# A hybrid decoder trunk: the opening, the S5 set-up and the S5 scan arranged in another way

## What is computed

```python
mod = (silu(c) @ ada_w[i] + ada_b[i])      # 6 parts of 1024: shift, scale, gate for mixer and FFN
hn = rms_norm(h, norm_mix_w[i]) * (1 + sc_m) + sh_m
proj = hn @ w_in                           # q, k, v, z, b/a (8 columns), u
# S5: 32 groups of 16 channels, each with 64 complex states
mag = exp(lr * dt); lb = mag * (cos(li * dt), sin(li * dt))
f = (lb - 1) / lam;  bb = f * b            # complex
x_t = lb * x_{t-1} + bb @ u_t              # complex scan over 512 steps
y = Re(c @ x) + d * u;  y = gelu(y);  y = y * sigmoid(y @ glu_w + glu_b)
# GDN: silu(causal conv of q, k, v), l2 norm, chunked delta rule, head norm, * silu(z)
out = concat(o_gdn, y_s5) @ w_out
```

## Time and profile before

| | us |
|---|---|
| runs | 1557.35, 1566.99, 1559.36 (median 1559.36) |
| the profiled execution | 1569.96, its span 1568.4, mean granted clock 0.909 |
| PE busy | 1415.3 (90%) |
| DVE busy | 771.9 (49%) |
| ACT busy | 503.9 (32%) |
| POOL busy | 215.3 (14%) |

### The profile page before, as it was taken

One profiled execution on the slowest core, in us unless ns is written; L12 is line 12 of the kernel. 1 busy time (PEld: TensorE's weight loads), 2 busy tenths in 40 slices (PEclk: granted clock), 3 DMA queues, 4 the chain that ended last, 5 costly groups with the idle time before them and its releaser, 6 DMA issues.

```text
span 1568.4 us, 17805 instructions
## 1 busy us (share of the span) xinstructions
PE 1415.3 (90%) x6956; PEld 1183.2 (75%) x6956; DVE 771.9 (49%) x762; ACT 503.9 (32%) x569; POOL 215.3 (14%) x256
## 2 busy tenths in 40 slices
PE   2479968968997899999999999999986999999997
PEld 1357857857996688888888878888775888888886
DVE  7792884065564646623366552444446323333243
ACT  3225320044413332212222234566524222222232
POOL 5891991034000000000000000000000000000000
PEclk6577985678999899989999979999997999999999
DMA  9117756310011447623374322211122232342321
GB/s 323 50 47 106 228 169 172 81 54 1 1 55 27 134 142 233 227 77 98 107 232 168 109 81 81 81 55 49 33 81 81 80 107 74 93 128 80 87 84 71
DMA packets 205705, 164.12 MB, mean 105 GB/s; under 512 B 29601, under 2 KB 195714, under 8 KB 203602
## 3 DMA queue, kind: packets, MB, share of 16 engines
q1 hardware_dynamic: 202416, 137.25, 30.7%
q0 software_dynamic: 2720, 25.99, 4.6%
q10 hardware_dynamic: 514, 0.12, 0.1%
HBM read 158.23 MB, written 4.19 MB: 104 GB/s over the span
## 4 chain that ended last, share of the span: by engine, by line
PE 78%; POOL 8%; DVE 6%; issue 4%; ACT 3%; DMA 1%; SPq 0%; DVEq 0%; ACTq 0%; POOLq 0%
PE banks L467 21%; PE banks L468 21%; PE banks L469 21%; PE banks L688 4%; DMA ada_first<-in_ada_w_dram 1%; DVE hn_lo L1547 1%; PE banks L659 1%; PE banks L661 1%; PE banks L922 1%; PE banks L949 1%; POOL scan_a L2107 1%; PE banks L663 1%; PE banks L542 1%; POOL scan_a L2108 1%; POOL scan_a L2102 1%
## 5 line engine op out<-in xcount | busy, mean ns | idle before, releaser
L467 PE MATMUL banks<-hn_hi,whi 128*128 128x512 f32 x992 | 393.0, 396 | 5.0 <-DVE hn_lo L1547 4.9
L468 PE MATMUL banks<-hn_lo,whi 128*128 128x512 f32 x992 | 390.6, 394 | 0.0
L469 PE MATMUL banks<-hn_hi,wlo 128*128 128x512 f32 x992 | 389.9, 393 | 0.0
L1515 DVE TENSOR_TENSOR wlo<-raw,whi 128x2048 fp32r<-128x2048 f32 (+3 forms) x107 | 232.0, 2169 | 145.0 <-ACT whi L1103 83.9
L467 PEld LDWEIGHTS banks<-hn_hi,whi 128*128 128x128 f32 x992 | 189.1, 191 | 48.4 <-issue 9.2
L1109 ACT ACTIVATE whi<-raw 128x2048 fp32r<-128x2048 f32 (+1 forms) x66 | 123.1, 1866 | 316.9 <-PE banks L469 315.8
L469 PEld LDWEIGHTS banks<-hn_hi,wlo 128*128 128x128 f32 x992 | 189.1, 191 | 40.2
L468 PEld LDWEIGHTS banks<-hn_lo,whi 128*128 128x128 f32 x992 | 189.3, 191 | 39.0
L467 PE MATMUL banks<-ff_hi,whi 128*128 128x512 f32 x416 | 163.9, 394 | 0.0
L469 PE MATMUL banks<-ff_hi,wlo 128*128 128x512 f32 x416 | 162.7, 391 | 0.0
L468 PE MATMUL banks<-ff_lo,whi 128*128 128x512 f32 x416 | 162.6, 391 | 0.0
(11 more groups left out here) (409 smaller groups left out, 1923.3 us busy)
## 6 DMA issues: line engine op xcount, KB each, us to landing
raw<-in_ffn_w_in_dram SPq DMA_DIRECT2D x88, 512.0 KB, 4.9
ada_in<-in_ada_w_dram POOLq DMA_DIRECT2D x16, 1536.0 KB, 6.4
ada_in<-in_ada_w_dram SPq DMA_DIRECT2D x32, 512.0 KB, 4.1
raw<-in_ffn_w_out_dram SPq DMA_DIRECT2D x32, 384.0 KB, 3.9
raw<-in_sb_w_in_dram SPq DMA_DIRECT2D x24, 512.0 KB, 4.4
raw<-in_hy_w_in_dram SPq DMA_DIRECT2D x20, 512.0 KB, 5.9
raw<-in_ffn_w_out_dram SPq DMA_DIRECT2D x32, 320.0 KB, 3.6
ada_first<-in_ada_w_dram SPq DMA_DIRECT2D x4, 2048.0 KB, 18.6
```

What stands on the lines that cost most here:

```text
L467: pe.matmul(o, lh, rh, start=first, stop=False)
L468: pe.matmul(o, lh, rl, start=False, stop=False)
L469: return pe.matmul(o, ll, rh, start=False, stop=last)
L1515: TTO(wlo[s][:, 0:width], raw[s][:, 0:width], whi[s][:, 0:width].bitcast(F32), SUB)\
```

## The change

1. `lam_raw` (16x128: lam_re, lam_im, dt) is turned by PE at once; DVE does everything on 128x16: 37 small instructions where there were 36 on 16x128, and after the sines another 29 (`lb`, `f`, powers), writing `pw_re`, `pw_im`, `f_co` itself. POOL's 29 instructions, PE's 18 turns and ACT's `powers` are gone. `sq` of x comes after this in DVE's list, and ACT's sines come ahead of its copies of x.
2. `c_raw` is loaded from ACT's queue; PE turns it after x's tile 3, ACT copies it after its tile 3 (`c_parts`). POOL then builds v in 12 instructions of half the size, waits for all of `hn`, zeroes `m_in`.
3. `ada_first` gets four tiles' room for all, 8 DMAs of 1 MB without a wait.
4. DVE makes `bb` right after the squares; after the norm come `w_rows(0, 0)`, `lo(2)`, `w_rows(0, 1)`, `lo(3)`, and `w_rows(1, ...)` between the conv blocks of q.
5. PE: u blocks 0 and 1 together, tile by tile of `hn` (`as_tiles_come`); b/a; u blocks 2, 3; then q's four blocks; then the taps, the gate sums, the 32 turns, p (three banks in turn instead of two); then k's and v's blocks.
6. The scan: each state is turned by a table (`turn_cos`, `turn_sin`, 128x1024 each) so that the recurrence is real; DVE does it in 12 instructions of 128x1024 and 32 `tensor_tensor_scan` of 128x64, in eleven pieces between the conv blocks of k and v. POOL's scan (120 instructions) goes; POOL makes the tables instead.
7. The tables and `scan_a`, `scan_b` lie over `ada0_in`. So SP waits for `scan_done` before tile 16 now, loads tiles 16 to 39, then `u_again`, `y_dram`, `y_s5`, then tiles 40 to 47, then slots 10, 11. DVE takes tiles 16 to 31 after the last conv block.
8. PE: `mod_parts(2)` between the third and fourth group of y, `mod_parts(4)` after both z slots.

```diff
@@ sync
-            for g in range(4):
-                if g == 3:
-                    sp.wait_ge(ada_used, 4)
-                rows = ada_w[0].rearrange("(p t) n -> p t n", t=8)[:, 4 * (g % 2):4 * (g % 2) + 4, :]
...
+            for g in range(8):
...
+            for n in range(4, 6):
+                load_slot(n, n % 2, cols(w, 256 * (n - 2))(n % 2))
             sp.wait_ge(u_out, 64)
-            sp.wait_ge(w_done, 8)
+            sp.wait_ge(v_done, 1)
...
-            for part in range(4, 6):
+            sp.wait_ge(scan_done, 1)
+            for part in range(2, 5):
                 for t in range(8):
                     ada0_tile(part, t)
-            sp.wait_ge(scan_done, 1)
...
+            for t in range(8):
+                ada0_tile(5, t)
             for s in range(2):
                 load_slot(10 + s, s, cols(s5_glu_w[0], 256 * s, k=4)(s))
@@ tensor
+            as_tiles_come(0, B_U, 0, (0, 1), lambda w_: w_[:, :].rearrange("p (k two m) -> p k two m", k=KT, two=2))
...
+            four_blocks(2, B_QKV, hn_hi, hn_lo)
             pe.wait_ge(bb_done, 1)
             pe.wait_ge(v_done, 1)
             for q in range(8):
-                b = 4 + q % 2
+                b = 4 + q % 3
...
-            with pe.Fori(0, 3) as i:
+            with pe.Fori(1, 3) as i:
                 four_blocks(2 + 2 * i, B_QKV + 4 * i, hn_hi, hn_lo)
-            mod_parts(2, ada0_acc, (24, 32))
...
             for q in range(4):
+                if q == 3:
+                    mod_parts(2, ada0_acc, (24, 32))
+                    pe.wait_ge(mod_done, 2)
...
+            z_blocks(0)
+            z_blocks(1)
+            pe.wait_ge(y_done, 4)
+            mod_parts(4, ada0_acc, (40, 48))
@@ scalar
+            act.preload_act_table(ACT.Silu)
+            qkv(0)
+            act.wait_ge(g_abs, 1)
+            step(act.activation(g_t[0][:, :, :], g_t[0][:, :, :], ACT.Exp, scale=-1.0))
+            act.activation(g_t[0][:, :, :], g_t[0][:, :, :], ACT.Ln, bias=ONE_C).then_inc(g_ln, 1)
+            act.activation(beta[:, :, :], ba[:, :, 0:NH], ACT.Sigmoid).then_inc(beta_done, 1)
+            act.wait_ge(m_zero, 1)
+            for q in range(8):
+                act.wait_ge(k_sum, q + 1)
...
@@ vector
+            for src, by, dst, n in ((1, 1, 2, 1), (1, 2, 3, 2), (1, 4, 5, 4)):
...
+            def states_turned(at_):
+                c_, s_ = turn_cos[:, :, :], turn_sin[:, :, :]
+                re, im, a, b = s_re[:, :, :], s_im[:, :, :], scan_a[:, :, :], scan_b[:, :, :]
+                def scans(dst, src, lo_):
+                    for i in range(lo_, lo_ + 8):
+                        last = dve.tensor_tensor_scan(dst[:, i, :], decay[:, i:i + 1].to_broadcast([P, NC]),
+                                                      src[:, i, :], 0.0, MUL, ADD)
+                    step(last)
+                if at_ == 0:
+                    dve.wait_ge(p_done, 4)
+                    dve.wait_ge(turn_done, 1)
+                    step(TTO(a, re, c_, MUL))
...
+                elif at_ == 10:
+                    TTO(re, b, a, SUB).then_inc(scan_done, 1)
...
+            for i in range(1, 3):
                 for r in range(4):
+                    if i == 1 and r == 0:
+                        states_turned(0)
+                    conv_block(i, r)
+                    for at_ in ((1, 2), (3,), (4, 5), (6,), (7,), (8,), (9, 10), ())[4 * i + r - 4]:
+                        states_turned(at_)
+            for part in range(2, 4):
+                for t in range(8):
+                    ada0_tile(part, t)
@@ gpsimd
+            for half in range(2):
+                ii = slice(8 * half, 8 * half + 8)
...
+            pool.wait_ge(hn_done, 8)
             pool.wait_ge(v_done, 1)
             pool.memset(m_in[:, :, :], 0.0).then_inc(m_zero, 1)
...
+            n = 1
+            while n < NC:
+                shape = [P, PAIRS, n]
...
+                step(tt(w_, s0, s_, MUL))
+                step(tt(c1, c0, c_, MUL))
+                step(tt(c1, c1, w_, SUB))
+                step(tt(w_, c0, s_, MUL))
+                step(tt(s1, s0, c_, MUL))
+                last = tt(s1, s1, w_, ADD)
+                n *= 2
+                if n < NC:
+                    step(last)
+                    doubled(turn_n)
+                else:
+                    last.then_inc(turn_done, 1)
```

More of the change, by code:

```diff
@@ L547, in _ @@
             pe.wait_ge(consts, 1)
+            pe.wait_ge(dt_done, 1)
+            for n in range(3):
+                last = pe.transpose(bank[5][:, 16 * n:16 * n + 16], lam_raw[:, n, :], ident[0:16, 0:16])
+            last.then_inc(lam_t, 1)
             pe.wait_ge(x_in, 16 * TT)
@@ L556, in _ @@
                 last.then_inc(x_t, 1)
-            norm(0)
+                if k == 3:
+                    pe.wait_ge(lam_exp, 1)
+                    pe.wait_ge(c_raw_in, 16 * 4)
+                    for part in range(2):
+                        for q in range(4):
+                            last = pe.transpose(bank[4 + part][:, q * P:(q + 1) * P], c_raw[:, part, q, :],
+                                                ident[:, :])
+                    last.then_inc(c_t, 1)
             pe.wait_ge(vec_in, 16 * 8)
@@ L584, in _ @@
             last.then_inc(ba_rows, 1)
-            four_blocks(0, B_U, hn_hi, hn_lo, first=True)
+            slot_ready(1)
+            for j in range(2):
+                gemm(2 + j, 1, j, hn_hi, hn_lo)
             pe.wait_ge(ba_copied, 1)
@@ L1059, in _ @@
             act.wait_ge(lam_in, 48)
-            act.activation(lam[:, 14, 0:2], lam[:, 14, 0:2], ACT.Exp).then_inc(dt_done, 1)
+            act.activation(lam_raw[:, 2, :].rearrange("i (two p) -> i two p", two=2),
+                           lam_raw[:, 3, 0:2].unsqueeze(2).to_broadcast([16, 2, GP]), ACT.Exp).then_inc(dt_done, 1)
+            for part, src in enumerate((s5_c_re, s5_c_im)):
+                rows = src[0].rearrange("(q g) h p -> (g h) q p", q=4)
+                for two in range(2):
+                    act.dma_start(c_raw[:, part, :, 64 * two:64 * two + 64], rows).then_inc(c_raw_in, 16)
             act.dma_start(vec_b[CONV:CONV + 48, :], hy_conv_w[0].rearrange("j (b p) -> (j b) p", p=P))\
@@ L1075, in _, with c_parts @@
             act.activation(c_act[:, :], c_col[:, :], ACT.Silu).then_inc(c_ready, 1)
+            def c_parts():
+                act.wait_ge(c_t, 1)
+                for par in range(2):
+                    rows = slice(64 * par, 64 * par + 64)
+                    for dst, b, scale in ((c_re, 4, 1.0), (nc_re, 4, -1.0), (nc_im, 5, -1.0)):
+                        src = bank[b].rearrange("p (i two h) -> p i two h", two=2, h=GH)[rows, :, par, :]
+                        last = act.activation(dst[rows, :, :], src, ACT.Copy, scale=scale)
+                last.then_inc(c_done, 1)
+            act.wait_ge(lam_exp, 1)
+            act.activation(lam[:, 11, :], lam[:, 8, :], ACT.Sin)
+            act.activation(lam[:, 10, :], lam[:, 7, :], ACT.Sin).then_inc(lam_trig, 1)
             for k in range(KT):
@@ L1619, in _ @@
+            w_rows(0, 0)
+            lo(2, 0)
+            w_rows(0, 1)
+            lo(3, 1)
             dve.wait_ge(ba_sum, 1)
@@ new lines, in conv_block @@
+            def conv_block(i, r):
+                dve.wait_ge(conv_tap, 4 * i + r + 1)
+                for s in range(1, 4):
+                    w_ = CONV + 12 * (3 - s) + 4 * i + r
+                    d_ = conv[:, i, r, s:T]
+                    last = STT(d_, bank[r][:, 0:T - s], vb[:, w_:w_ + 1], d_, MUL, ADD)
+                    if s < 3:
+                        step(last)
+                last.then_inc(block_free, 1)
+                if r == 1:
+                    lo(4 + 2 * i, 0)
+                if r == 3:
+                    lo(5 + 2 * i, 1)
@@ L2001, in _ @@
                         .then_inc(bc_in, 16)
-            for part, src in enumerate((s5_c_re, s5_c_im)):
-                rows = src[0].rearrange("(q g) h p -> (g h) q p", q=4)
-                for two in range(2):
-                    pool.dma_start(c_raw[:, part, :, 64 * two:64 * two + 64], rows).then_inc(bc_in, 16)
             pool.dma_start(w_ba[:, :, :], hy_w_in[0][:, 4 * W:4 * W + 8].rearrange("(k p) n -> p k n", p=P))\
```

488 lines of the change are left out of this document (209 added, 279 removed).

## The result

The changed kernel takes 1581.65 us (median of three runs, 1578.72 to 1584.71) against 1559.36: 1.2% slower, ratio 1.0122 [1.0082, 1.0162]. Forecast were 1567 and a range up to 1582, so the time lies 0.35 us inside the range's upper end, and on the slower side of the 1% bound, to which I had given 0.20. The profiled execution is the one of 1584.71, its span 1583.1.

A forecast was written before the change was run, and what follows sets the result against it. Only the part before the first GDN product can change, where PE waited 21.2 us for POOL's scan. `scan_done` 220.2 + tail 114 = 334 against 326.4, +7.8 us; on the median 1559.36 that gives 1567, range 1542 to 1582.

The forecast's parts named there:

- 1% bound: Whole kernel: slower by over 1%, above 1575 us, was given a chance of 0.20.
- S: The time of `scan_done`, forecast at 220.2 us; the steps behind it are counted from there.
- ACT's `c_parts` lets POOL begin at 29.7: Opening: ACT's copies of c_raw are done so that POOL starts the v build at 29.7 us.
- to 23.2: Opening: DVE's 37 and 29 small steps, 9.3 + 6.4 us from 7.5 on, end at 23.2.
- The port: Opening: POOL's v build and DVE's two-input instructions take turns on the SBUF port, from 29.7 to 64.8 us.
- the rival of a less strict one: Opening: DVE slips in two instructions per POOL instruction, norm up to 15 us sooner, time 1552; chance 0.12.
- p to scan_done: DVE's scan, conv blocks, `lo` and a wait for k: 49.1 us instead of 89.8, `scan_done` at 220.2.
- From the gate step to p: Taps, gate sums, turns and p on PE at the low clock, from 142.8 to `p_done` at 171.1 us.
- The tail: From `scan_done` to the GDN sums: tiles at 2.8 us and the y path on SP's list, 114 us, +28.7.
- The rival "the tiles hide": Behind `scan_done`: a tile takes 1.9 us, the 24 tiles save 22 us, time 1545; chance 0.13.
- The first rival (tables late): POOL's scan tables ready only at 197 us, DVE waits, `scan_done` 21.5 us later, time 1588; chance 0.15.
- a dear scan (+12): DVE's 32 scan instructions, 6.7 us with bounds 4 to 19; the dear case sets the range's high side.

The follow-up runs named there:

- Run 1: The changed kernel with the four c_raw loads moved from ScalarE's queue back to GpSimd's; 1574.74 us, ratio 1.0081 to the kernel before.
- run 3: The changed kernel with GpSimd's v build waiting until the norm is done; 1570.28 us, ratio 1.0039 to the kernel before.
- run 6: The changed kernel with a third buffer for the condition's tiles; 1574.01 us, ratio 1.0057 to the kernel before.
- runs 5 and 12: 5: the changed kernel with all scan steps at once, 1586.1 us. 12: run 11 with two z blocks in front of y, 1532.63 us.
- run 8: The changed kernel itself, measured again as the base; 1582.45 us, ratio 1.0125 to the kernel before.
- run 11: The changed kernel with c_raw on GpSimd's queue, v build behind the norm, third tile buffer, y path behind all tiles; 1539.31 us.

## Why the prediction came out as it did

Step by step, forecast against the profile after:

| step | forecast | measured |
|---|---|---|
| VectorE's powers end | 23.2 | 32.4 |
| v build | 29.7 to 64.8 | 38.6 to 73.2 |
| norm end | 93.5 | 101.3 |
| last u block | 111.3 | 120.7 |
| first `m_in` copy after the gate step | 142.8 | 152.0 |
| `p_done` | 171.1 | 177.8 |
| tables ready | 157 | 157.8 |
| `scan_done` | 220.2 | 226.0 |
| tile 31, 40 used | S + 46, + 87 | S + 45, + 87.5 |
| first sum of squares | S + 114 = 334 | S + 115.9 = 342.0 |

- **The step that failed** is "ACT's `c_parts` lets POOL begin at 29.7", and ahead of it the 66 steps "to 23.2": I let the powers run through without pricing ScalarE's queue, on which the sines stand behind the four c_raw loads. The change moves these DMAs, and I counted them as nothing. Run 1 shows the term: 8 to 9 us, and with it put in, the forecast for the first sum is 342 to 343, against 342.0.
- **The port** was right, and the rival of a less strict one wrong: a tile of 1.28 takes 3.3 beside GpSimd, and the v build took 34.6 us (35.1 forecast). The Trainium skill says in "GPSIMD Engine Reference", in the table at its head, that the SBUF interfaces are shared and contended for where VectorE has two SBUF inputs; run 3 agrees, 3.26 against 1.28 us, and the addition of the squares 2.7 against 0.68. What I did not ask is who needs v: nobody before the taps at 150. The 24 us at the norm, of which 17 are left at `scan_done`, were to be had by one wait, and theory A of run 3 still had the opening set by the powers and the loads.
- **p to scan_done** was 48.3 us against 49.1; the scans 6.3 us against 6.7, the products 1.23 each. From the gate step to p the forecast was 2.5 too long, since the clock was back at 1.00 from 170 us on, where I had taken the low one for all turns. The tables were ready as forecast partly by luck: GpSimd began them 4 us late (101.4 against 97) and took 56.4 us instead of 60.
- **The tail** was right in size and in cause: SyncE's list, tiles at 2.64 to 2.8 us, u_again and y in the middle. The rival "the tiles hide" failed. Its 1.9 us a tile exists, but it takes a third buffer (run 6). The first rival (tables late) didn't occur here; in run 3 it is just reached. Two small sums of the prediction are off, 29.5 less five times 0.6 is 26.5 and not 26.7, and 111.3 + 21.9 is 133.2 and not 133.6; nothing hangs on them.
- **Beyond the profile** there are 22.3 us between the medians where the profiled executions are 14.7 apart. The profiled execution of before was 10.6 above its median, and I took that excess for something the change does not touch. That was an assumption: behind the first sum this profile is as long as all others (1242.0), so the excess may as well lie in front of it, in the stretch that changes. The other executions of before were not profiled and their spread is wide (1553.6 to 1572.0 over the later runs), so the cause of this half of my miss, 7.5 of 14.7 us, stays open.
- **The range** held, and by luck. Its upper end stood on a dear scan (+12), and the scan was slightly cheaper than forecast. What brought the time up there were ScalarE's queue and the 7.5 us between profiles and medians, and neither was among its terms.

In parts: p comes 26.4 us later than before (177.8 against 151.4), from there to `scan_done` 41.5 are won (48.3 against 89.8), and the tail costs 30.6 more (115.9 against 85.3). So the change loses because its gain of 15 us at `scan_done` (23 in run 1, without the queue's term) is smaller than the 31 us of tiles and transfers that it sends behind `scan_done`. With c_raw's queue, the place of the v build, a third buffer and the order behind `scan_done` changed, a kernel with this scan is 2% faster than the one before; how much of that the kernel before would gain from the same edits was not tried.

Not tried either: the mod sum at another place between the y groups, and a y that keeps the full clock beyond its first 5 us (runs 5 and 12).

## What to carry to other kernels

A DMA issue is an instruction of the engine that issues it: price it at the time for which it holds that engine, which here rose from 0.4 to 8.1 us once other loads were ahead of it in the same queue, and look at what stands behind it. Where two engines share a port, ask who needs the slower one's result and start it after the other one's chain, not as early as its inputs allow. And when work is pulled forward in a list with fixed posts (a sum between two groups, transfers between two parts), find the next post first; until it is moved, speed in front of it is worth nothing.

## What was not expected of the hardware

- Two DMAs of 512 packets of 256 bytes each (128 KB) held ScalarE's queue for 8.69 us, and a following one of 24 KB held it for 4.57. The price is not one per load: the first three of the four c_raw loads took 0.40 to 0.54 us, the fourth alone 8.13 (view of the tile `c_raw`, min/median/max ns below). All DMAs together moved some 400 GB/s up to 13 us and 206 to 278 from there to 21. ScalarE's queue carried 2112 more packets than before, 2048 of them c_raw's (behind the tile's row: queue and kind, packets, MB, share; before, then after):

```profile
L1064 ACTq DMA_DIRECT2D c_raw<-in_s_c_im_dram x2: 532/4332/8131, 7.9 to 8.5; - x2
```
```profile
q10 hardware_dynamic: 514, 0.12, 0.1%
```
```profile
q10 hardware_dynamic: 2626, 0.64, 0.2%
```
  From GpSimd's queue the same four took 0.77 to 0.80 us each (run 1). Full DMA engines alone don't make it dear: in run 1 ScalarE's eight small loads took 0.26 to 0.58 us each, between 6.8 and 10 us, while 412 GB/s were moved. Small packets are not needed for it: SyncE's two loads of 512 KB issued at 5.2 us took 7.75 us, and two of the same kind at 104.7 us 0.92. What the dear ones share is a queue that had been given much just before. That this is the reason is a guess; no run varied it.
- A `tensor_tensor_scan` over 64 columns takes 0.196 us (8 in 1.57). The Trainium skill has it at half throughput ("DVE: opcode table, instruction layouts, handler registers and perf-mode slots", Datapath and trigger behaviour); with one width measured, no run here tells a rate from a fixed part.
- The pace of a double-buffered load of 512 KB was (load 4.3 + use 1.3)/2 = 2.8 us, some 190 GB/s; with a third buffer (4.5 + 1.3)/3 = 1.9 (1.8 measured). It is a rule of thumb: in run 8 the median load was 3.8 us and the pace 2.7, not 2.55.
- TensorE's clock fell from 1.00 to 0.50 about 5 us into y in runs 5 and 12 (at 237.4 and 217.6 us), although it was busy without a gap, with products of 64 and 63 columns behind blocks of 512. With a wait of 5.3 us in front of y it was at 0.50 from y's first product (run 11).
